# Attention outputs: VectorE makes the scaled copy, ScalarE squares it in SBUF; the exponential's table is loaded in the projection

## What is computed

```python
def diff_attention(q, k, v, lam):
    ...
    s = jnp.einsum('bqhcd,bkhcd->bhcqk', qblk, k).astype(F32)
    p = jax.nn.softmax(s, axis=-1)
    att = p[:, :, 0] - lam * p[:, :, 1]
    return jnp.einsum('bhqk,bkhe->bqhe', att.astype(v.dtype), v)
...
    o = diff_attention(q * DIFF_D ** -0.5, keys, vals, lam)
    o = head_rms_norm(o, NORM_EPS) * lp['diff_gn_g'] * (1.0 - lam_init)
```

## Time and profile before

| | us |
|---|---|
| median of 3 runs | 2035.12 (2035.07 to 2035.83) |
| the profiled execution, its own time | 2041.96 |
| the profiled execution, its span | 2039.7 |
| busy: PE / PEld | 1928.3 / 1736.8 |
| busy: DVE / ACT / POOL | 1036.8 / 712.6 / 34.4 |
| projection ends, attention starts, layer 0 / layer 1 | about 488 / 1494 |
| attention ends, layer 0 / layer 1 | about 529 / 1534 |

### The profile page before, as it was taken

How to read it: one execution, slowest core, us unless ns; L and a number is a source line. 1 busy time by engine, 2 the same in 40 slices (tenths; PEclk the granted TensorE clock), 3 DMA queues, 4 the chain that set the end, 5 groups by cost and what they waited for, 6 DMA issues and landing times.

```text
span 2039.7 us, 37391 instructions
## 1 busy us (share of the span) xinstructions
PE 1928.3 (95%) x16214; PEld 1736.8 (85%) x16214; DVE 1036.8 (51%) x1629; ACT 712.6 (35%) x1192; POOL 34.4 (2%) x69
## 2 busy tenths in 40 slices
PE   6999999998899899999999999999988789999996
PEld 5899997987669779999979999989866787899996
DVE  2333335655556675333365333366547758633336
ACT  3322223445533343222243222245364324422221
POOL 0000000000000001000000000000000000000000
PEclk8999999998888898999999999999999799999998
DMA  7733336333571044333344333323335003433320
GB/s 323 294 125 125 128 130 233 118 110 124 235 321 40 26 165 160 129 125 123 124 165 145 123 123 123 124 84 124 105 137 219 11 4 124 168 124 123 123 103 31
DMA packets 41472, 277.71 MB, mean 136 GB/s; under 512 B 4778, under 2 KB 6810, under 8 KB 9344
## 3 DMA queue, kind: packets, MB, share of 16 engines
q1 hardware_dynamic: 35424, 255.34, 34.7%
q0 software_dynamic: 3312, 16.91, 2.1%
q10 hardware_dynamic: 2608, 3.56, 0.5%
HBM read 269.22 MB, written 3.41 MB: 134 GB/s over the span
## 4 chain that ended last, share of the span: by engine, by line
PE 82%; DVE 11%; ACT 4%; issue 2%; DMA 1%; ACTq 0%; PEld 0%; PEldq 0%; SPq 0%; POOL 0%; DVEq 0%; POOLq 0%
PE bank L918 17%; PE bank L983 17%; PE bank L922 17%; PE bank L921 17%; PE bank L758 2%; DMA ring<-weights 1%; PE bank L1371 1%; PE bank L1360 1%; PE bank L1378 1%; DVE ring_r L2160 1%; DVE ln_stat L2179 1%; PE bank L767 1%; PE bank L839 1%; DVE x L2177 1%; DVE arena L2170 1%
## 5 line engine op out<-in xcount | busy, mean ns | idle before, releaser
L2160 DVE TENSOR_TENSOR ring_r<-ring,arena_r 128x1024 fp32r<-128x1024 f32 x328 | 387.8, 1222 | 705.8 <-ACT arena_r L1649 705.3
L918 PE MATMUL bank<-arena_r 128*128 128x384 f32 (+3 forms) x2056 | 700.8, 341 | 13.3 <-DVE arena_r L2209 11.2
L922 PE MATMUL bank<-arena_r,ring_r 128*128 128x384 f32 (+2 forms) x1816 | 604.8, 333 | 0.0
L921 PE MATMUL bank<-arena_r 128*128 128x384 f32 (+2 forms) x1816 | 602.9, 332 | 0.0
L918 PEld LDWEIGHTS bank<-arena_r 128*128 128x128 f32 x2056 | 391.7, 191 | 35.4 <-issue 19.8
L1649 ACT ACTIVATE arena_r<-ring 128x1024 fp32r<-128x1024 f32 x340 | 340.5, 1052 | 138.3 <-PE bank L922 136.7
L921 PEld LDWEIGHTS bank<-arena_r 128*128 128x128 f32 x1816 | 343.5, 189 | 3.5
L922 PEld LDWEIGHTS bank<-arena_r,ring_r 128*128 128x128 f32 x1816 | 343.4, 189 | 0.0
L983 PE MATMUL bank<-arena_r 128*128 128x512 f32 x1128 | 310.9, 393 | 0.3 <-issue 0.3
L1780 ACT ACTIVATE arena<-bank 128x384 f32<-128x384 f32 x88 | 43.3, 492 | 740.1 <-PE bank L922 740.1
L983 PEld LDWEIGHTS bank<-arena_r 128*128 128x128 f32 x1128 | 210.7, 188 | 42.2 <-issue 1.2
(11 more groups left out here) (294 smaller groups left out, 1832.2 us busy)
## 6 DMA issues: line engine op xcount, KB each, us to landing
ring<-weights SPq DMA_DIRECT2D x242, 1024.0 KB, 4.9
lnrow<-ln_in POOLq DMA_DIRECT2D x6, 1024.0 KB, 6.0
const<-consts POOLq DMA_DIRECT2D x1, 2211.0 KB, 9.5
arena<-gate POOLq DMA_DIRECT2D x4, 385.0 KB, 7.9
x<-x_in ACTq DMA_DIRECT2D x1, 1536.0 KB, 13.7
rows<-row_in POOLq DMA_DIRECT2D x2, 704.0 KB, 10.4
par<-par_in POOLq DMA_DIRECT2D x2, 662.5 KB, 7.5
y_out<-x SPq DMA_DIRECT2D x2, 512.0 KB, 2.6
```

Of the source, the lines that this page charges most:

```text
L918: mm = pe.matmul(out, w_h, h_h, start=start, stop=False, skip_group_check=True)
L921: pe.matmul(out, w_h, h_l, start=False, stop=False, skip_group_check=True)
L922: return pe.matmul(out, w_l, h_h, start=False, stop=stop, skip_group_check=True)
L2160: ve.tensor_tensor(low_unit((l, name), u) if out is None else out, raw, place.bitcast(F32), ALU.subtract).then_inc(w_ready, 1)
```

## The change

Three things are edited. ScalarE's program gets one more activation, an exponential of a single column of constants, right behind `tokm_read(1, 2)`, so that the table load falls there and not at the first exponential of the attention; its result, `table_col`, is not read. VectorE's program gets the scaled copy out of bank 7, `outputs(i - 4)` ahead of `maxima(i)`, the last three behind `gla_distance(0)` and ahead of `gla_scale(0)`; it raises `att_out`. ScalarE's `outputs` waits for `att_out`, not `att_mm`, and squares the copy in `mixed`; its own copy is gone.

```diff
--- before.py
+++ after.py
@@ -532,6 +532,7 @@
         ln_r = small[:, 183:192].rearrange("p (g n) -> p g n", g=GROUPS)
         diff_gn = lnrow[:, 1, 0:P]
         eps_col = small[:, 176:177]
+        table_col = small[:, 162:163]
 
 
         arrived = [sem(f"arrived{s}", True) for s in range(RING)]
@@ -1888,6 +1889,8 @@
                                 round_tokm(m + HI_PROJ)
                             if end:
                                 tokm_read(q, 2)
+                            if end and q == 1:
+                                sc.activation(table_col, eps_col, ACT.Exp)
                             if m == 0:
                                 sc.wait_ge(gla_b_ready, 1)
                             if m < 3:
@@ -1919,11 +1922,9 @@
 
                         def outputs(u):
                             g, h = u // HEADS, u % HEADS
-                            sc.wait_ge(att_mm, u + 1)
-                            own.link(sc.activation(squares_tmp, ps[7][:, 0:P], ACT.Square, scale=att_r[:, u, 0:1],
+                            sc.wait_ge(att_out, u + 1)
+                            own.link(sc.activation(squares_tmp, mixed[:, g, 512 + h * P:512 + h * P + P], ACT.Square,
                                                    accum_out=diff_ss[:, u:u + 1]))
-                            sc.activation(mixed[:, g, 512 + h * P:512 + h * P + P], ps[7][:, 0:P], ACT.Copy,
-                                          scale=att_r[:, u, 0:1]).then_inc(att_out, 1)
 
                         for i in range(GROUPS * HEADS + 3):
                             if i < GROUPS * HEADS:
@@ -2480,12 +2481,22 @@
                             ve.scalar_tensor_tensor(att[:, b, 0:n], e_sb[:, b, 1, 0:n], att_ratio[:, b:b + 1], e_sb[:, b, 0, 0:n],
                                                     ALU.mult, ALU.add).then_inc(weights_ready, 1)
 
+                        def outputs(u):
+                            g, h = u // HEADS, u % HEADS
+                            ve.wait_ge(att_mm, u + 1)
+                            ve.tensor_scalar(mixed[:, g, 512 + h * P:512 + h * P + P], ps[7][:, 0:P], att_r[:, u, 0:1], None,
+                                             ALU.mult).then_inc(att_out, 1)
+
                         for i in range(GROUPS * HEADS + 1):
+                            if i >= 4:
+                                outputs(i - 4)
                             if i < GROUPS * HEADS:
                                 maxima(i)
                             if i >= 1:
                                 weights(i - 1)
                         gla_distance(0)
+                        for u in range(GROUPS * HEADS - 3, GROUPS * HEADS):
+                            outputs(u)
                         gla_scale(0)
 
                     def gla():
```

## The result

| | before | after |
|---|---|---|
| median, us (7 runs each) | 2035.12 (2028.09 to 2038.89) | 2022.76 (2021.43 to 2029.3) |
| ratio, 95% interval | | 0.9937 (0.9916 to 0.9958) |
| profiled execution: time, span | 2041.96, 2039.7 | 2029.3, 2027.0 |
| mean granted clock of that execution | 0.968 | 0.973 |

The change is faster by 12.4 us on the medians, where 4.8 was forecast. One execution of the early load alone took 2418 us at a mean granted clock of 0.739, where all the others had 0.965 or more; it is left out of its mean.

The account below looks back on a forecast made before the run. TensorE, 82% of the chain, was taken to bound the kernel. Load 2.60, ring 2.0, tail 0.54 and clock -0.3 summed to 4.8 us off 2035.12: 2030.3 us, range 2027.5 to 2033.7.

Parts of the forecast that it names:

- The load: Exponential's table load at each attention's start, moved into ScalarE's idle stretch: first exponential 1.30 us earlier, twice, 2.60 us.
- rival C: A table load holds ScalarE longer than its row, and that goes too: gain 7.6 us, 2027.5; chance 0.03.
- The ring: Mid-attention chain repeating every two units, 5.37 us: value product no longer waits for ScalarE's square and copy; 2.0 us gained.
- an unhindered value product: TensorE's value product in the attention, taken to start 0.56 us after its turn's start when nothing delays it.
- the walk: Following the new order from the weights' copy's end, 510.51: transposes at 510.64, value product at 511.20, not 511.40.
- Nine waits in the list: TensorE's waits for ScalarE's scaled copy (L1925): 2.4 us, 9 times over both layers, 0.03 to 0.05 taken off each.
- VectorE's copy at nothing: VectorE's added scaled copies in the attention, 0.40 us each, twelve a layer, were to delay no maxima: no cost.
- The tail: Attention's end: without ScalarE's copy the last gate copies start about 0.27 us earlier; 0.54 us for both layers.
- The clock: TensorE's 1.2 GHz dip in the attention: work pulled forward into it runs slower; a quarter of the loss booked, -0.3 us.
- Rival B: The attention's clock dip shortens or fails to come in one layer: gain 7.4 us, 2027.7; chance 0.14.
- The forecast's base and range: Same 4.8 us taken off the 2035.12 median, giving 2030.3; range 2027.5 to 2033.7 from the steps' bounds.

Follow-up runs that it names:

- both of the later profiles: The changed kernel as it is, run and profiled twice more: 2026.96 us, ratio 0.9961, and 2025.69 us, ratio 0.995.
- the ten products: Changed kernel plus ten unread matrix products in TensorE's idle time before each attention's first turn: 2023.9 us, ratio 0.9954.
- the second profile of before: The kernel before, nothing changed, profiled and timed once more: 2035.13 us median, ratio 1.0006; its profiled execution took 2028.41 us.

## Why the prediction was wrong, step by step

**The load, 2.60: right.** 1.26 us a layer at equal clock, 2.52. The Trainium skill's page "ScalarE: Activation LUTs", section "What ACT_TABLE_LOAD costs", would have had 2.66 a layer go; the trace does not agree, and rival C falls with it.

**The ring, 2.0: mis-sized.** The step that failed is "from the start of a turn to that of an unhindered value product is 0.56 (513.10 to 513.66)": that product was hindered, and an unhindered one comes 0.36 behind its turn. So the product of the walk starts at 511.00, not 511.20, and the wait is worth 0.40, not 0.20: the 0.23 of idle time on TensorE's timeline is only what the modelled end of the turn left of it. The two units take 4.95, not 5.17. Nine waits in the list was not the right count either, but the chain crosses fewer and not more, eight. Eight times 0.39 make 3.1 us. From the attentions' lengths, 2.97 a layer less 1.26 for the load and 0.25 for the tail leave 1.46, 2.9 us for both layers; VectorE's copy on the chain where the large units begin is a cost that lies in this 2.9.

**VectorE's copy at nothing: nearly right.** From the ring's even part on no maxima of the chain wait for it. Where the large units begin they do three times, by 0.3 us at most: the prediction set the copy against the 0.88 of TensorE's scores, but VectorE comes to it only behind its weights' pass. The Trainium skill's page "Advanced Engine Details and Errata", section "The Read-Write Bubble", that spoke against it: VectorE's pass from the bank took 0.350 where ScalarE's had 0.37, and ScalarE's square from SBUF 0.31 where the one from the bank had 0.38. The square also lost its scale by a column, so its 0.06 is not the crossing's price alone. No loss from either crossing is to be seen here.

**The tail, 0.54: right.** 2.89 to 2.64, 0.25 a layer.

**The clock, -0.3: wrong in sign and by far in size.** In the attention the dip of layer 0 shrank from 10.2 to 6.8 us in both of the later profiles too; in layer 1 it came out at 3.4, 6.8 and 10.2; 3.4 us of it cost 0.2 to 1.1. Rival B named this with 2.3 a layer for no dip at all; the ten products measured 1.4. But the greater part lies outside. The prediction booked nothing for the clock in the stages between and behind the attentions. Over the runs the mean granted clock was 0.9730 before (118 runs) and 0.9768 after (31), and among the runs of one and the same kernel an execution with 0.001 more was 1.1 us shorter: about 4 us. 5.9 + 4 is 9.9, measured were 9.4. This sum is a correlation, not a cause shown: which stretches get the dips differs from one execution to the next.

**The forecast's base and range: the second failed step.** "Nothing in these stretches explains the offset" of 6.8 us between the profiled execution and the median was true and should have warned me: the second profile of before puts the offset down to the clock, most of it between the attentions. The three times of before lay within 0.8 us of each other, the 125 within 17. The lower end of the range, 2027.5, was built from bounds of the steps and held nothing of that. (By the prediction's own terms, B with the ring in full is a gain of 7.8, 2027.3.) That the first comparison came out 5 us under it was in part luck of the draw; but the mean of all runs, 2026.4, is below it too. At equal clock the terms sum to 5.9 us, not far over the 5.1 of load, ring and tail.

## What to carry to other kernels

Before taking a row as "without a wait", look up when every engine it could wait for had ended: a constant distance (here 0.14 us) behind another engine's end is a wait, even where the trace shows no idle time, since merged rows have modelled ends. Then look whether the chain crosses that wait at all: here it crossed eight of 13, and these set the gain. In such a ring, give the bank back before any work that can read the copy; which engine copies matters only when that engine's time, not the round of waits, sets the pace. And where the granted clock moves between executions of one kernel, compare stretches at equal clock and take a second profile of before, since a single one may differ by more than the change.

## What I had not expected of the hardware

- Two executions of the same kernel had 58 and 24 us at 1.2 GHz between 530 and 800 us, and differed by 13.5 us in time.
- In the attention, 3.4 us more at 1.2 GHz cost from 0.2 us (37.96 to 38.19) to 1.1 (39.45 to 40.53). The two profiles of before with 10.2 us of it differ by 0.7 us, one dip against two pieces; what decides the cost is not shown.
- VectorE's scaled 128x128 pass from a bank took 0.350 us here and 0.402 in the line of the earlier trace rows; the traces do not tell why.
